# Two attention stages of a two-network kernel: heads paired by layout, two weight buffers, a new order of the steps

## The reference

```python
# sliding: 16 query heads of 64, 2 key/value heads, window 128
q = rms_norm(q, q_gain); k = rms_norm(k, k_gain); q, k = rope(q), rope(k)
scores = q @ k_band / 8            # blocks of 128 queries, 256 keys
m = max(max(scores), sink); p = exp(scores - m)
o = (p / (sum(p) + exp(sink - m))) @ v_band ; x = x + o @ w_out
# banded: 16 query heads, 4 key/value heads, 512 tokens + 256 context keys
s = concat(q @ kc, where(mask, q @ k_band, -1e30)) / 8
p = softmax with a sink ; o = (p_ctx @ vc + p_band @ vb) * silu(g) ; x = x + gate_x * (o @ w_o)
```

## Time and profile before

| | before |
|---|---|
| median of 3 runs | 3206.78 us (3196.72 to 3207.16) |
| profiled execution | 3198.47 us, span 3196.4 us |
| TensorE, VectorE, ScalarE, GpSimd busy | 92%, 48%, 37%, 3% |
| mean granted TensorE clock | 0.954 of full speed |
| chain that ended last | PE 83%, DVE 8%, ACT 5%, issue 3% |
| HBM | 73 GB/s over the span |
| sliding stage | 1500.7 to 1706.9 us |
| banded stage | 2675 to 3129 us |

### The profile page before, as it was taken

One profiled execution on the slowest core, in us unless ns is written; L12 is line 12 of the kernel. 1 busy time (PEld: TensorE's weight loads), 2 busy tenths in 40 slices (PEclk: granted clock), 3 DMA queues, 4 the chain that ended last, 5 costly groups with the idle time before them and its releaser, 6 DMA issues.

```text
span 3196.4 us, 38949 instructions
## 1 busy us (share of the span) xinstructions
PE 2926.6 (92%) x14436; PEld 2367.3 (74%) x14436; DVE 1531.1 (48%) x2168; ACT 1168.6 (37%) x1825; POOL 88.5 (3%) x90
## 2 busy tenths in 40 slices
PE   7999999989999999999778999989999978877767
PEld 2588888878888888887567888867888867665556
DVE  2344326664443254434564444245666654444444
ACT  2322225664322142223443332134555533333332
POOL 1000000000000000000000000001101000100000
PEclk9999999999999999999988999989999978988878
DMA  8433321122333233332001333321111101100001
GB/s 306 136 98 92 105 86 54 54 57 79 92 95 102 92 95 98 95 98 90 27 27 58 98 95 94 104 60 40 40 39 39 40 27 47 33 27 14 27 20 53
DMA packets 333667, 234.28 MB, mean 73 GB/s; under 512 B 6952, under 2 KB 308112, under 8 KB 333584
## 3 DMA queue, kind: packets, MB, share of 16 engines
q1 hardware_dynamic: 332672, 231.63, 24.0%
q0 software_dynamic: 912, 1.53, 0.2%
HBM read 231.04 MB, written 2.10 MB: 73 GB/s over the span
## 4 chain that ended last, share of the span: by engine, by line
PE 83%; DVE 8%; ACT 5%; issue 3%; DMA 0%; ACTq 0%; SPq 0%; DVEq 0%
PE ps L441 23%; PE ps L443 22%; PE ps L442 22%; PE ps L719 3%; PE ps L695 3%; PE ps L1059 2%; PE ps L1196 2%; DVE bw_pt_l L2425 1%; ACT apr L1818 1%; PE ps L822 1%; PE ps L1031 1%; DVE wl L436 1%; DVE bw_pr L2417 1%; ACT sw_pr L1566 1%; PE ps L826 1%
## 5 line engine op out<-in xcount | busy, mean ns | idle before, releaser
L441 PE MATMUL ps<-act_h,wl 128*128 128x512 f32 x2224 | 896.8, 403 | 19.4 <-DVE tmp L2271 16.2
L442 PE MATMUL ps<-act_l,wh 128*128 128x512 f32 x2224 | 874.2, 393 | 0.0
L443 PE MATMUL ps<-act_h,wh 128*128 128x512 f32 x2224 | 873.9, 393 | 0.0
L436 DVE TENSOR_TENSOR wl<-raw,wh 128x1024 fp32r<-128x1024 f32 x382 | 459.8, 1224 | 510.2 <-ACT wh L432 504.4
L432 ACT ACTIVATE wh<-raw 128x1024 fp32r<-128x1024 f32 x382 | 392.5, 1050 | 421.9 <-PE ps L443 347.6
L441 PEld LDWEIGHTS ps<-act_h,wl 128*128 128x128 f32 x2224 | 423.5, 190 | 111.6 <-DVE tmp L2271 18.2
L442 PEld LDWEIGHTS ps<-act_l,wh 128*128 128x128 f32 x2224 | 423.4, 190 | 89.5 <-issue 6.2
L443 PEld LDWEIGHTS ps<-act_h,wh 128*128 128x128 f32 x2224 | 422.4, 190 | 90.7
L441 PE MATMUL ps<-h_h,wl 128*128 (+1 forms) x704 | 277.4, 394 | 0.0
L443 PE MATMUL ps<-h_h,wh 128*128 (+1 forms) x704 | 276.0, 392 | 0.0
L442 PE MATMUL ps<-h_l,wh 128*128 (+1 forms) x704 | 273.2, 388 | 0.0
(11 more groups left out here) (350 smaller groups left out, 3898.3 us busy)
## 6 DMA issues: line engine op xcount, KB each, us to landing
raw<-in_ffn_w_gate_up SPq DMA_DIRECT2D x176, 512.0 KB, 4.0
raw<-in_ffn_w_down SPq DMA_DIRECT2D x88, 512.0 KB, 3.7
mod_raw<-in_w_mod SPq DMA_DIRECT2D x12, 2048.0 KB, 8.0
raw<-in_a_w_in SPq DMA_DIRECT2D x32, 512.0 KB, 4.1
raw<-in_sb_w_in SPq DMA_DIRECT2D x24, 512.0 KB, 3.9
raw<-in_b_w_in SPq DMA_DIRECT2D x20, 512.0 KB, 3.8
raw<-in_w_o SPq DMA_DIRECT2D x16, 512.0 KB, 3.9
raw<-in_sw_w_in SPq DMA_DIRECT2D x10, 512.0 KB, 4.0
```

The source lines that it names most:

```text
L436: dve.tensor_tensor(wl[:, slot, :], raw[:, slot % RAWS, :], f32(wh[:, slot, :]), ALU.subtract).then_inc(lo_done[slot], 1)
L441: pe.matmul(bank, w_lo, r_hi, start=start, stop=False, skip_group_check=skip)
L442: pe.matmul(bank, w_hi, r_lo, start=False, stop=False, skip_group_check=skip)
L443: return pe.matmul(bank, w_hi, r_hi, start=False, stop=stop, skip_group_check=skip)
```

## The change

- A host-side reordering of weight columns, output rows and sinks (`laid_out`) puts heads c and c+8 into one 128-row chunk. They use key heads 0 and 1 in the sliding stage, so k and v are used as they come, and no duplicating matmul is left. In the banded stage a pair uses one of two key pairs (`c // 4`).
- The probabilities get two buffers in both stages (`sw_pr` by chunk, `bw_pr` by step). An exponential waits for transposes two steps back.
- Sliding: jobs of q (norm, rope) run three chunks ahead and alternate between two pairs of temporary buffers; half 2 is projected in the lead. The projection, rotation and mean move within a chunk; the split of a weight half is for c+4, and on ScalarE it stands behind the exponentials. The cosine product and the sum of rope go to GpSimd.
- Banded: loop weights use four slots instead of two; the query is projected two pairs ahead and the gate in its own pair. Values are taken by head. Silu is tanh on ScalarE and one more operation on VectorE, so that one table set serves the loop.
- The splits of halves 2 and 3 of the differential and the banded stage go into the norm stage before, ahead of the x norm.

```diff
-    plan.stage("band", lead=4, fixed=2, times=8)
+    plan.stage("band", lead=4, fixed=4, times=4)
...
     elif st.kind == "band":
         for t in range(4):
             ring_load(st, w_b_in[:, :, bass.ds(D_MODEL + 256 * (t % 2) + P * (t // 2), P)], t)
-        with sp.Fori(0, 8) as i:
-            for t in range(2):
-                loop_load(st, w_b_in[:, :, bass.ds(i * P + t * 1536, P)], t, i, 2)
+        for n in range(-1, 8):
+            if n >= 0:
+                loop_load(st, w_b_in[:, :, bass.ds(1536 + n * P, P)], 2 * (n % 2) + 1, n // 2, 4)
+            if n < 7:
+                loop_load(st, w_b_in[:, :, bass.ds((n + 1) * P, P)], 2 * ((n + 1) % 2), (n + 1) // 2, 4)
...
+    def rope(job):
+        a_, b_ = tmp[:, job % 2 * 2, :], tmp[:, job % 2 * 2 + 1, :]
+        pool.wait_ge(w.rot, base.rot + job + 1)
+        pool.tensor_tensor(a_, a_, sw.cos[:, :], ALU.mult).then_inc(w.rc, 1)
+        pool.wait_ge(w.t2, base.t2 + job + 1)
+        pool.wait_ge(w.rc, base.rc + job + 1)
+        pool.tensor_tensor(b_, b_, a_, ALU.add).then_inc(w.rp, 1)
...
+    pool.wait_ge(trig, 4)
+    for job in range(9):
+        rope(job)
...
     def turned(c, e):
         pe.wait_ge(w.pn, base.pn + 2 * c + e + 1)
...
-                src = sw.pr[:, 4 * e + j, (1 - which) * P:(2 - which) * P]
+                src = sw.pr[:, c % 2, 4 * e + j, (1 - which) * P:(2 - which) * P]
                 last = pe.transpose(psf[:, col:col + P], src, fconst(F_IDENT))
...
     def chunk(c):
         scores(c)
-        if c < 7:
-            rotate(c + 2, 6)
+        if c == 0:
+            rotate(2, 5)
+        if c < 6:
+            head_mean(c + 3, 7)
         if c:
             turned(c - 1, 0)
-        if c < 6:
-            pe.wait_ge(w.t2, base.t2 + c + 3)
-            project(pe, *query_half(c + 2), ps[:, 6, :], act_h, act_l, ks=range(0, 4))
+        if c < 5:
+            pe.wait_ge(w.qs, base.qs + c + 3)
+            project(pe, *query_half(c + 3), ps[:, 6, :], act_h, act_l, ks=range(0, 4))
         if c:
             turned(c - 1, 1)
         if c < 6:
-            project(pe, *query_half(c + 2), ps[:, 6, :], act_h, act_l, ks=range(4, 8))
+            rotate(c + 3, 7)
+        if c < 5:
+            project(pe, *query_half(c + 3), ps[:, 6, :], act_h, act_l, ks=range(4, 8))
         if c:
             values(c - 1)
-        if c < 6:
-            head_mean(c + 3, 6)
...
-    transposes(4, lambda b: sw.pr[:, 2 + b // 2, b % 2 * P:(b % 2 + 1) * P], NBLK).then_inc(w.vtr, 1)
+    transposes(4, lambda b: sw.pr[:, 0, 2 + b // 2, b % 2 * P:(b % 2 + 1) * P], NBLK).then_inc(w.vtr, 1)
+    pe.wait_ge(w.qs, base.qs + 1)
+    project(pe, *query_half(1), ps[:, 6, :], act_h, act_l, ks=range(0, 4))
     rotate(0, 2)
-    pe.wait_ge(w.qs, base.qs + 1)
-    project(pe, *query_half(1), ps[:, 6, :], act_h, act_l)
-    head_mean(1, 5)
-    pe.wait_ge(w.rp, base.rp + 1)
-    for g in range(2):
-        pe.matmul(ps[:, g, :], fconst(F_DUP0 + g), tmp[:, 3, :], start=True, stop=True).then_inc(w.dup, 1)
-    rotate(1, 2)
-    head_mean(2, 6)
+    head_mean(1, 0)
+    project(pe, *query_half(1), ps[:, 6, :], act_h, act_l, ks=range(4, 8))
+    pe.wait_ge(w.qs, base.qs + 2)
+    project(pe, *query_half(2), ps[:, 7, :], act_h, act_l, ks=range(0, 4))
+    rotate(1, 3)
+    project(pe, *query_half(2), ps[:, 7, :], act_h, act_l, ks=range(4, 8))
+    head_mean(2, 5)
     for c in range(8):
         chunk(c)
     turned(7, 0)
...
     def query(c, ks):
-        if 0 in ks:
-            pe.wait_ge(w.gs, base.gs + c)
-            pe.wait_ge(w.t2, base.t2 + c + 2)
-        slot, n = loop_half(st, 0, c)
+        if 0 in ks and c > 1:
+            pe.wait_ge(w.gs, base.gs + c - 1)
+        slot, n = loop_half(st, 2 * (c % 2), c // 2)
         last = part(slot, n, ps[:, 6, :], act_h, act_l, ks)
         if KT - 1 in ks:
             last.then_inc(product[slot], 1)
 
     def gate(c, ks):
         if 0 in ks:
-            pe.wait_ge(w.t2, base.t2 + c + 3)
-        slot, n = loop_half(st, 1, c)
+            pe.wait_ge(w.gs, base.gs + c)
+            pe.wait_ge(w.t2, base.t2 + min(c + 4, 10))
+        slot, n = loop_half(st, 2 * (c % 2) + 1, c // 2)
         last = part(slot, n, ps[:, 6, :], act_h, act_l, ks)
         if KT - 1 in ks:
             last.then_inc(product[slot], 1)
...
     def pair(c):
-        more = c < 7
         scores(c, 1)
+        if c < 7:
+            rotate(c + 3, 0, 6)
         if c:
-            values(c - 1, 1)
-        if more:
-            query(c + 1, range(0, 2))
+            values(c - 1, 1, 0)
         turned(c, 0, 0)
-        if more:
-            query(c + 1, range(2, 4))
+        if c:
+            values(c - 1, 1, 1)
+        gate(c, range(0, 1))
         turned(c, 0, 1)
+
         scores(c, 2)
-        if more:
-            query(c + 1, range(4, 6))
+        gate(c, range(1, 3))
         turned(c, 1, 0)
-        if more:
-            query(c + 1, range(6, 8))
+        gate(c, range(3, 6))
         turned(c, 1, 1)
+        gate(c, range(6, 8))
+
         scores(c, 3)
-        if more:
-            rotate(c + 3, 0, 6)
-        values(c, 0)
-        if more:
-            gate(c + 1, range(0, 2))
+        values(c, 0, 0)
         turned(c, 2, 0)
-        if more:
-            gate(c + 1, range(2, 4))
+        values(c, 0, 1)
+        if c < 6:
+            query(c + 2, range(0, 2))
         turned(c, 2, 1)
-        if more:
+
+        if c < 7:
             scores(c + 1, 0)
-            gate(c + 1, range(4, 6))
+        if c < 6:
+            query(c + 2, range(2, 4))
         turned(c, 3, 0)
-        if more:
-            gate(c + 1, range(6, 8))
+        if c < 6:
+            query(c + 2, range(4, 6))
         turned(c, 3, 1)
+        if c < 6:
+            query(c + 2, range(6, 8))
...
     for t in range(4):
         part(*half(st, t), ps[:, t, 0:CTX], actc_h, actc_l, norm=mc if t == 0 else None).then_inc(w.pc, 1)
-    for t in (0, 2, 1, 3):
+    for t, bank in ((0, 4), (2, 5), (1, 4), (3, 5)):
         slot, n = half(st, t)
-        part(slot, n, ps[:, 4 + t, :], act_h, act_l, norm=mx if t == 0 else None).then_inc(product[slot], 1)
-        if t == 2:
-            rotate(0, 0, 4)
         if t == 1:
-            copies(0)
-            rotate(1, 1, 6)
-    copies(1)
+            rotate(0, 0, 6)
+        if t == 3:
+            rotate(1, 1, 7)
+        part(slot, n, ps[:, bank, :], act_h, act_l, norm=mx if t == 0 else None).then_inc(product[slot], 1)
+    pe.wait_ge(w.t2, base.t2 + 1)
+    query(0, range(KT))
     v_turned(0)
-    slot, n = loop_half(st, 0, 0)
+    v_turned(1)
     pe.wait_ge(w.t2, base.t2 + 2)
-    part(slot, n, ps[:, 6, :], act_h, act_l).then_inc(product[slot], 1)
-    v_turned(1)
-    rotate(2, 0, 6)
-    slot, n = loop_half(st, 1, 0)
-    part(slot, n, ps[:, 7, :], act_h, act_l).then_inc(product[slot], 1)
+    rotate(2, 0, 7)
+    query(1, range(KT))
     scores(0, 0)
     for c in range(8):
         pair(c)
-    values(7, 1)
+    values(7, 1, 0)
+    values(7, 1, 1)
...
+    if st.mod and not who_c:
+        for t in (2, 3):
+            split_hi(act, *half(st.following, t))
     act.wait_ge(ms_done, START + m + 1)
...
-        act.wait_ge(w.tr, base.tr + 2 * c)
+        if c > 1:
+            act.wait_ge(w.tr, base.tr + 2 * (c - 2) + e + 1)
...
     def chunk(c):
-        if c < 7:
-            head_root(c + 2, 6)
+        if c < 6:
+            head_log(c + 3, 7)
         if c:
             p_hi(c - 1, 0)
-        if c < 7:
-            split_hi(act, *loop_half(st, (c + 3) % 2, (c + 3) // 2))
+        if c < 6:
+            head_root(c + 3)
         exponentials(c, 0)
         if c:
             p_hi(c - 1, 1)
...
         if c < 7:
             q_hi(c + 1)
         if c < 6:
-            squared(c + 3)
+            split_hi(act, *loop_half(st, c % 2, (c + 4) // 2))
+        if c < 5:
+            squared(c + 4)
         if c:
             out_hi(c - 1)
...
-        slot, n = loop_half(st, 1, c)
+        slot, n = loop_half(st, 2 * (c % 2) + 1, c // 2)
         act.wait_ge(product[slot], START + n + 1)
-        if c > 1:
-            act.wait_ge(w.og, base.og + c - 1)
-        act.activation(bw.gs[:, c % 2, :], ps[:, 6 if c else 7, :], ACT.Silu).then_inc(w.gs, 1)
-        act.preload_act_table_set(LN_EXP)
+        act.wait_ge(w.og, base.og + c)
+        act.activation(bw.gs[:, :], ps[:, 6, :], ACT.Tanh, scale=0.5).then_inc(w.gt, 1)
 
     def exponential(c, j, e):
-        W = len(BW_TILES[j]) * P
-        act.wait_ge(w.nm, base.nm + 4 * c + j + 1)
-        if c or j:
-            act.wait_ge(w.tr, base.tr + 8 * c + 2 * j + e - 1)
-        act.activation(bw.pr[:, e, 0:W], psf[:, e * 1024:e * 1024 + W], ACT.Exp, bias=bw.nm[:, e:e + 1],
-                       scale=SCALE, accum_out=bw.den[:, e:e + 1]).then_inc(w.pe, 1)
+        n, W = 4 * c + j, len(BW_TILES[j]) * P
+        act.wait_ge(w.nm, base.nm + n + 1)
+        if n > 1:
+            act.wait_ge(w.tr, base.tr + 2 * (n - 2) + e + 1)
```

(99 more changed lines are left out.)

363 lines of the change are left out of this document (185 added, 178 removed).

## The result

The changed kernel takes 3032.47 us (median of four runs, 3030.34 to 3034.6) against 3201.75 us for the kernel before on the same chip: ratio 0.9471, 95% interval 0.9448 to 0.9494. The forecast was 3039 us. The profiled execution took 3030.34 us.

What follows compares the result with a forecast made beforehand. TensorE, busy 92% of the span, bounds the kernel, so only its waits can be regained: 124 + 17 + 12 + 10 = 163 us off 3198.5 gives 3035.5, plus 3.5 for timed runs, 3039 us; own range 3017 to 3062, with rivals 3016 to 3090.

Steps and rivals of the forecast that it cites:

- Banded pairs: Banded loop over eight head pairs: a pair falls from 45.3 to 31.5 us, bound by TensorE's work; 124 us less.
- the walk over the four steps: Banded pair: the dependency chain followed step by step against TensorE's new order, concluding that TensorE's own work is the bound.
- the second ring: Banded pair: scores, bound, a VectorE extra, low part, transpose, copy, low part; meets TensorE's work within 0.7 us each step.
- the ring: Banded loop before: exponentials wait 208.3 us for transposes of the step before; a second probability buffer was to end this.
- Starts of the two stages: Differential and banded stages: splitting halves 2 and 3 before the x norm gains 12 us each; banded lead 17 in all.
- Sliding: Sliding stage: lead 6.1 us earlier, chunk 0 -1.3, chunks 1 to 5 -1, chunks 6 and 7 +6.6; 10 us gained.
- The trap: Sliding chunks 1 to 5: VectorE's weight split, queued before a low part, follows ScalarE's late half; TensorE waits 3.8 us.
- clock 1.0 us a chunk: Sliding chunks 1 to 5: 1.0 us added to each for TensorE's lower clock with a longer idle piece.
- The first: Rival, 22%: banded pairs stay a ring of waits at 38 us, six pairs lose 39 us, total 3078 us.
- The clock in the loop: Rival, 8%: 30% of banded loop time stays at the lower clock, pairs take 36.5 us, total 3069 us.
- Tanh and the exponential share their table: Rival, 3%, said they don't: two table loads a banded pair remain on ScalarE, up to 21 us, total 3060 us.
- GpSimd's hold on VectorE: Rival, 5%: GpSimd's rope operations stop VectorE in the sliding stage, 20 us, stage 10 us slower than before, total 3059.

Runs made afterwards that it cites:

- experiment 6: Changed kernel with the banded loop's gate projections in one pass instead of three (16 of 24 matmuls a pair left out): 3031.45 us, ratio 0.9463.
- Experiments 4: Changed kernel with one buffer of probabilities in the banded stage instead of two: 3064.77 us, ratio 0.9564.
- 12: Changed kernel with one banded probability buffer and the values of both heads ahead of the first transposes again: 3103.66 us, ratio 0.9689.
- experiment 7: Changed kernel with Silu in the banded gate instead of tanh, with two table loads a pair: 3035.27 us, ratio 0.9475.
- Experiment 5: Changed kernel with the third and fourth weight halves split at the top of the differential and banded stages again: 3057.44 us, ratio 0.9543.
- experiment 3: Changed kernel with the sliding stage's two rope operations (cosine product, sum) back on VectorE instead of GpSimd: 3039.14 us, ratio 0.9484.
- experiment 11: Changed kernel with VectorE's low-half weight split later in the sliding chunks and rope's cosine product and sum on VectorE: 3000.63 us, ratio 0.9366.

## Why the prediction was right, and where not

**Banded pairs: right in kind and nearly in size.** Said: 31.5 us for pairs 0 to 5, 29.5 and 35 for the last two, 124 us gained. Measured: 29.2, five of 30.56, 27.9 and 36.2, 131.4 gained. TensorE's own work sets the pair, as the walk over the four steps gave it, and the estimate 30.4 to 31.3 drawn from busy time and clock was the right one. The walk had the second ring within 0.7 us of TensorE's work, and experiment 6 shows how close that is: 3.4 us of matmuls less, and the pair is no shorter.

**What opened the ring: incomplete.** The prediction gave it to the second buffer. Experiments 4 and 12 measure 34.5 us for the buffer, and 40.1 for the values taken by head while there is one buffer. What is left of the 131 us, 56 us, was not taken apart; the places of query and gate, their four slots, and the clock that goes with them (0.84 in the earlier trace rows, 0.86 over the loop of experiment 12) are in it. Silu and its loads are not, as far as experiment 7 shows it in the new order.

**Starts of the two stages: right.** Said 12 us in the differential stage and 17 in the banded. Against the start of each norm stage, the first x projection comes 11.8 us earlier, and the first scores of the banded loop 17.6. Experiment 5 gives 25 us back for the splits alone, for 24.

**Sliding: the mechanism right, two chunk times put too low.** The lead is 6.1 us earlier, as said; chunk 0 grew by 1.4 for 1.3; the last chunk with its end gained 3.1 for 3.3. But chunks 1 to 5 take 105.5 us, 3.2 more than before where I had 1, and chunk 6 takes 16.0 instead of 14.2, at clock 0.69. Sum: no gain in the chunks where I had 4, and 6 us in the stage where I had 10. VectorE's 5.15 us and TensorE's 3.74 of waiting are those of the prediction (5 and 3.8).

**The trap cost more than its price.** In the sum it stood at 3.8 us of waiting, 1.0 of clock and 0.4 beside GpSimd, 5.2 a chunk. Taking the wait away gave 34.1 us in the sliding loop (164.25 to 130.17): 6.2 us for each of chunks 1 to 5, since TensorE then works at clock 1.00 in the middle chunks, and 3.2 in chunk 0. The term "clock 1.0 us a chunk" was a difference to the kernel before, which had the lower clock too: 0.95 over chunks 1 to 5, where the changed kernel has 0.84.

**The rivals.** The first did not come: pairs of 30.56 us are no ring of 38. The clock in the loop went from 0.84 to 0.97. Tanh and the exponential share their table: one load ahead of the loop and none in it. GpSimd's hold on VectorE is there in single operations but does not decide: with or without its work chunks 1 to 5 take the same time, with the stall (experiment 3) and without it (experiment 11).

**The signs.** Most of those named ahead came: no idle stretch of 9 us before either stage, VectorE idle some 5 us a chunk, chunks of 19.8 to 22.3 us for 19 to 21, pairs 30.56 us apart for 31 to 32. Two did not. A pair under clock 0.9 was to mean wrong, and the last pair has 0.81; VectorE's waits for copies were to be small, and are 35.0 us in the loop, from 113.2. Neither weighs in the sum: the last pair took 36.2 us for 35.

**The number.** The time came 6.5 us under the forecast. 4.9 of it are in the span, 167.9 us shorter for 163: 7.4 more from the pairs, 3.9 less from the sliding stage, 1.4 for small differences elsewhere. Most of the rest is what I had allowed between the profiled and the timed runs, 3.5 us, where it was 2.1. That the total is this close is in part luck, as the misses of the pairs and of the sliding stage have opposite signs.

## What to carry to other kernels

Where an in-order engine has a wait for another engine's side work (a weight split) ahead of work on the path, move either end of it: here 32 of 3032 us for one line, with no cost that showed. Price a recurring idle piece with the clock it brings, not by its length: read the busy time of the same matmuls in stretches at both levels. And "the engine is 97% busy" does not say that less work would help: look how close the next ring stands before cutting. Before a difference of a few microseconds is put down to an edit, compare the stretches one by one: in experiment 3 most of it lay where the edit had changed nothing. Whether the sliding stage needs its second buffer once the stall is gone was not tried.
